# Where the attention loop of a decoder kernel copies a finished output tile on ScalarE

## The reference, cut to what matters

```python
def dilated_attention_mixer(h, positions, w_in, w_out):
    ...
    for gi, (window, dil) in enumerate(DILATED_GROUPS):      # (128,1), (512,4), (2048,16)
        q = (rotary(proj[:, :, gi, 0], positions) * scale).transpose(0, 2, 1, 3)
        k = rotary(proj[:, :, gi, 1], positions).transpose(0, 2, 1, 3)
        v = proj[:, :, gi, 2].astype(jnp.float32).transpose(0, 2, 1, 3)
        o, lse = dilated_window_attention(q, k, v, window, dil)
        ...
    wts = jax.nn.softmax(jnp.stack(lses), axis=0)
    o = jnp.sum(wts[..., None] * jnp.stack(outs), axis=0)
    ...
    return o @ w_out
```

## Time and profile before

| | us |
|---|---|
| median of 3 runs | 2744.57 |
| lowest, highest run | 2738.52, 2748.45 |
| profiled execution, its own time | 2748.45 |
| its span | 2746.7 |
| mean granted TensorE clock over the span | 0.965 of full |
| TensorE matmuls busy in the span | 2539.1 (92%) |
| ScalarE busy in the span | 672.6 (24%) |

### The profile page before, as it was taken

One profiled execution on the slowest core, in us unless ns is written; L12 is line 12 of the kernel. 1 busy time (PEld: TensorE's weight loads), 2 busy tenths in 40 slices (PEclk: granted clock), 3 DMA queues, 4 the chain that ended last, 5 costly groups with the idle time before them and its releaser, 6 DMA issues. The chain is left out here.

```text
span 2746.7 us, 37869 instructions
## 1 busy us (share of the span) xinstructions
PE 2539.1 (92%) x13849; PEld 1387.3 (51%) x13850; DVE 1016.5 (37%) x2302; ACT 672.6 (24%) x1468; POOL 337.2 (12%) x390
## 2 busy tenths in 40 slices
PE   6999999999999999999986999999799999999995
PEld 2665656656764433433332566575784433333332
DVE  2443354443443322212225445444443323222216
ACT  1031030311312222222222333433312222222221
POOL 0101001010001111111100122121101111111110
PEclk9999999999999999999997999999899999999998
DMA  7525235152539999999963031221446899999966
GB/s 278 187 63 160 85 109 171 58 171 90 195 132 343 372 419 421 412 412 403 412 258 112 31 92 50 73 74 33 147 178 251 340 419 420 406 420 413 406 248 275
DMA packets 177816, 654.94 MB, mean 238 GB/s; under 512 B 26884, under 2 KB 88684, under 8 KB 122504
## 3 DMA queue, kind: packets, MB, share of 16 engines
q1 hardware_dynamic: 112752, 394.89, 36.9%
q10 hardware_dynamic: 29784, 149.13, 14.2%
q0 software_dynamic: 35136, 109.10, 11.2%
HBM read 614.18 MB, written 53.52 MB: 243 GB/s over the span
## 5 line engine op out<-in xcount | busy, mean ns | idle before, releaser
L1462 DVE TENSOR_SCALAR core_oT<-moe_tx,moe_by,moe_plus 128x128 f32<-128x128 f32 x360 | 123.0, 404 | 668.2 <-PE moe_tx L1709 668.0
L675 PE MATMUL attn_proj<-core_hT,core_ring 128*128 128x512 f32 x768 | 334.4, 596 | 8.6 <-ACTq L497 5.2
L1734 PE MATMUL moe_ph<-weights_w,core_oT 128*32 128x512 f32 (+2 forms) x1216 | 314.2, 628 | 14.8 <-issue 14.8
L1748 PE MATMUL moe_py<-weights_w,moe_hT 128*32 128x512 f32 (+2 forms) x1296 | 312.7, 596 | 0.9 <-ACT moe_hT L1186 0.9
L1734 PE MATMUL moe_pr<-weights_w,core_oT 128*64 128x512 f32 (+2 forms) x864 | 271.2, 597 | 3.5 <-issue 3.5
L675 PEld LDWEIGHTS attn_proj<-core_hT,core_ring 128*128 128x128 f32 x768 | 146.5, 191 | 188.9 <-issue 183.2
L2395 PE MATMUL gdn_pj<-core_hT,core_ring 128*128 128x512 f32 x512 | 226.9, 598 | 0.0
L1269 POOL DMA_INDIRECT y_rows<-moe_ysb,moe_yidx x90 | 95.0, 1055 | 953.5 <-ACT moe_ysb L1199 704.7
L1186 ACT COPY moe_hT<-moe_th 128x256 f32<-128x256 f32 x90 | 33.6, 374 | 660.5 <-PE moe_th L1697 660.5
L671 PE MATMUL attn_proj<-core_ring,core_hT 128*128 128x256 f32 x768 | 176.5, 391 | 0.0
L671 PEld LDWEIGHTS attn_proj<-core_ring,core_hT 128*128 128x128 f32 x768 | 169.3, 282 | 11.2 <-issue 3.8
(11 more groups left out here) (410 smaller groups left out, 3458.0 us busy)
## 6 DMA issues: line engine op xcount, KB each, us to landing
weights_w<-in_expert_w_dram SPq DMA_DIRECT2D x160, 1024.0 KB, 15.5
weights_w<-in_expert_w_dram ACTq DMA_DIRECT2D x92, 1024.0 KB, 10.3
core_ring<-in_expert_w_dram SPq DMA_DIRECT2D x54, 1024.0 KB, 15.7
core_hT<-in_expert_w_dram SPq DMA_DIRECT2D x48, 1024.0 KB, 13.8
core_ring<-in_attn_w_in_dram SPq DMA_DIRECT2D x36, 1024.0 KB, 7.3
weights_w<-y_rows SPq DMA_DIRECT2D x32, 1024.0 KB, 13.0
core_ring<-in_expert_w_dram ACTq DMA_DIRECT2D x30, 1024.0 KB, 10.4
attn_ada_w<-in_ada_w_dram POOLq DMA_DIRECT2D x64, 384.0 KB, 5.9
```

Source lines behind the costliest of these rows:

```text
L675: last = nc.tensor.matmul(proj[n % 2][:], w[:, j % SLOTS, kk, half_ * P:(half_ + 1) * P], c.hT[:, kk, :], start=kk == 0, stop=kk == KT - 1)
L1462: last = nc.vector.tensor_scalar(xT[:, b, k], tx[1][:, k - 4], by[:, k:k + 1], plus[:, k:k + 1], ALU.mult, ALU.add)
L1734: last = nc.tensor.matmul(ph[p % 2][at, :], xT[:, p % 2, k, at], w13[ew.up_place(n)[0]][:, :, k], start=k == 0, stop=k == KT - 1)
L1748: last = nc.tensor.matmul(py[n][at, :], hT2[:, p % 2, k, at], w2[ew.down_place(m)[0]][:, k, half(n)], start=k == 0, stop=k == 1)
```

## The change

In the loop that issues ScalarE's work of the softmax part, `turned_out(step - 3)` moves from behind the step's first exponential to the end of the step. Before, a step's order on ScalarE was exponent(step, 0), turned_out(step - 3), turned(step - 1, 0), exponent(step, 1), turned(step - 1, 1). After, it is exponent(step, 0), turned(step - 1, 0), exponent(step, 1), turned(step - 1, 1), turned_out(step - 3). Nothing is added or taken away, and no other engine's program changes.

```diff
                 for step in range(PAIRS + 3):
                     for hh in range(2):
                         if step < PAIRS:
                             exponent(step, hh)
-                        if hh == 0 and 0 <= step - 3:
-                            turned_out(step - 3)
                         if 0 <= step - 1 < PAIRS:
                             turned(step - 1, hh)
+                    if 0 <= step - 3:
+                        turned_out(step - 3)
```

## The result

The changed kernel takes 2763.62 us (median of 6 runs, 2762.27 to 2770.67), the kernel before 2743.71 (median of 6, 2738.52 to 2748.45): a ratio of 1.0078, 95% interval 1.0067 to 1.0088, slower by 20 us. The forecast was 2758.6, within 2749 to 2771.

A forecast was written before the change was run, and what follows sets the result against it. The prediction took a serial chain through TensorE, with ScalarE outside its loop, to bound the kernel. Terms of 0.61 + 0.69 + 1.47 + 0.72 = 3.5 us a turn, 14.0 in four, added to 2744.6 gave 2758.6, range 2749 to 2771.

The forecast's parts named there:

- Where the loop closes before: Settled softmax steps before the change: a loop through TensorE and VectorE, 3.62 us a step, with ScalarE not in it.
- First late start: Start of a turn's softmax part: values(1), waiting for turned_out, starts 0.61 us late, more than the 0.34 of cover.
- The new loop: Settled steps after the change: ScalarE comes into the loop, 3.85 us a step (3.82 to 3.89) in place of 3.62.
- its copy 0.70 later: Term of the settled step after the change: ScalarE's copy of head 0 starts 0.70 us after its transposition starts.
- Where the cover is gone: End of a turn, no scores left: values(5) need a whole ScalarE step after values(4), 3.85 for 2.38, 1.47 us more.
- The last step: End of a turn: turned_out(5) stands behind both copies of item 7, so values(6) follow values(5) 0.72 us later than before.
- Sum of the waits: All late starts of a turn's softmax part together: 3.5 us a turn, 14.0 us in four turns.
- Clock as before: Whole kernel: TensorE's granted clock stays as it was, so only the 14 us of waits are added; chance 0.63.
- the prediction's own last sign: The forecast is wrong if the clock's row at the end of turns 1 to 3 shows 1.2 GHz.
- rival A: TensorE's clock falls too at the ends of three turns: 3 us each, 9 together, 2767.6 us; chance 0.21.
- Rival B: The clock's fall at the start of turns 1 to 3 goes away: at most 15 us back, 2744 to 2753; chance 0.12.
- The likeliest case by itself: Whole kernel, waits of 12.5 to 14.6 us and a few us for how runs fall: 2753 to 2763 us.

The follow-up runs named there:

- late_tail: Kernel before with turned_out last in its step only in steps 7 and 8, two of a turn's eight copies: 2753.48 us, ratio 1.0039.
- the two parts measured apart: Kernel before with turned_out last only in steps 3 to 6 (2747.91 us), and with it last only in steps 7 and 8 (2753.48 us).
- late_two_pv: Changed kernel with values and turned_out taking two PSUM tiles in turn instead of the single pv tile: 2742.42 us, ratio 0.9994 to the kernel before.
- before_start_half: Kernel before with extra 128x256 TensorE matmuls, results unused, in the holes at the start of each softmax part: 2742.39 us, ratio 1.0003.

## Why the prediction was right, and where it was short

- *Where the loop closes before.* Right: with the copy one place later (middle_place) steps stay at 3.62 and nobody waits, so ScalarE was not in the loop.
- *First late start, 0.61.* 0.57: in turn 4 values(1) follow values(0) by 4.19 in place of 3.62.
- *The new loop, 3.85 a step (3.82 to 3.89).* Right in its members, 3.91 in size, just outside my bounds. The term that was mis-sized is "its copy 0.70 later": it measured 0.77 (365.96 to 366.73), and the two transpositions now load in one run. The exponential behind the copy, taken as 0.50, measured 0.48. The lateness grows by 0.29 a step (0.57, 0.86, 1.16, 1.45 in turn 4), where 0.23 was forecast.
- *Where the cover is gone, 1.47.* 1.52 (3.90 less 2.38), and 1.81 where it stands alone in late_tail, as no earlier step has paid for the late place there.
- *The last step, 0.72.* 0.82, in turn 4 of the changed kernel (2.97 to 3.79) and in late_tail.
- *Sum of the waits, 14.0.* 0.57 + 0.88 + 1.52 + 0.82 = 3.79 a turn, 15.1 in four; 15.8 by the times of the two parts measured apart; all by the single tile (late_two_pv: nothing left against the kernel before).
- *Clock as before.* This step failed, and by the prediction's own last sign: the clock's row at a turn's end does show 1.2 GHz. I named the holes and priced them at 0 to 15 us as rival A, and took none into the forecast, because the gaps there today leave the clock up. That premise held for turns 1 to 3 of the profile it was read from; behind turn 4 the same profile has the clock at half (0.50 from 712.2 to 715.5 us), and before_start_half, with the old order too, has it behind its turn 3 (0.52 from 538 to 541.2). With the new holes the falls are more: the clock fell at the end of turn 2 and behind turn 1 in one profile, at the ends of turns 2 and 4 and behind turn 3 in the other. Over many runs it is 16 us more at half clock, 3 to 8 us of time by the traces and the estimate. The Trainium skill's rule on short idles ("TensorE: Matmul & The Clock Gate", "A second HAM failure mode: psum-queue depth-cycling"), which I had quoted for it, agrees with these traces: a granted clock of 0.50 from 382 to 390 us, behind holes of at most 2.03 us.
- *Rival B* was there in one profile: from 184 to 189 us, at the start of turn 1, the granted clock is 0.99 in the first profile of the changed kernel and 0.50 in that of before. In the second it is 0.50 again, so for this turn it was luck, as the prediction had it. The fall in turn 3 costs less in both (1.3 and 1.4 us above the full-clock length, 2.8 before). It didn't outweigh A.
- *The number.* The likeliest case by itself reached to 2763, and the kernel came out at its edge, 2763.6: 20 us more where 14 were forecast. The range held because it took in part of A. The mechanism of the waits was right; that the total lies near the forecast owes nothing to the clock step.

## What to carry to other kernels

A copy that empties a single accumulator is part of the loop of the engine that fills it, however idle the copying engine is: find the moment at which the next writer asks for the tile, count what stands ahead of the copy, and price it step by step, the last steps of a loop by themselves, since there the cover (here the scores) is missing and two of eight copies made two thirds of the waits. A second tile takes the order out of the sum. And new holes of one to two us in TensorE's work can have a second price through the clock. It is read turn by turn against the lengths at full clock, and over many runs from the mean clock, rather than from the spans of one pair of profiles. A test that adds instructions to a loop needs a look at the instruction queue, as it may change the loop's jump as well.

## What the runs showed of the hardware that I had not expected

- TensorE's clock fell at 382 us although no single hole of its loads ahead of that was longer than 2.03 us (1.79 for its matmuls), and stayed at half to about 396, over a tail and over projections that left no gap from 389.6 on.
- The spread of the runs of this kernel (2734 to 2753 us over the 80 of before) goes mostly with the clock: correlation 0.91 between time and us at half clock. Yet before_start_half, with 16 us less at half clock, was no faster.
- With a few matmuls more in the loop, the jump back to its head took 4.1 us in one turn and 0.63 in another of the same execution; the instruction queue q8 moved a packet in each of five such long jumps and in none of the four short ones.
